# Retention's output in buffers of its own, branch A's finish on VectorE one block per pair of heads, and 32-row tiles for sample states and gate's low-rank rows

## What is computed

```python
z = rmsnorm(x) @ w_in                               # 1024 -> 6944 columns
za, zb, ga, gb = z[:SHIFT_W], z[SHIFT_W:...], ...   # branch A, branch B, two merge gates
# branch A: RWKV-7, 8 heads of 64
zs = za + mu * (shift(za) - za)
r, k, v, dw, da, dg = split(zs)                     # dw 64, da 64, dg 160 columns: low rank
decay = exp(-exp(-softplus(-(w0 + tanh(dw) @ lw_up)) - 0.5))
a = sigmoid(a0 + da @ la_up)
g = sigmoid(dg) @ lg_up                             # 160 -> 512
S = S * decay - (S kk) b^T + v k^T;  y_t = S r_t     # over tokens, done in chunks of 64
ya = (head_norm(y) * gain + bias + (r . k r_k) v) * g
# branch B: retention, 8 heads, keys of 64, values of 128
o = chunkwise_retention(rotary(q), rotary(k) / 8, v, S_ret)
yb = head_norm(o) * silu(gate)
x = x + rmsnorm((sigmoid(ga) * (ya @ w_out_a) + sigmoid(gb) * (yb @ w_out_b)) @ w_o)
x = x + rmsnorm((silu(h @ w_gate) * (h @ w_up)) @ w_down)          # h = rmsnorm(x)
```

## Time and profile before

| | |
|---|---|
| median of 3 runs | 1299.23 us (1298.85 to 1300.09) |
| profiled execution | 1297.91 us |
| its span in the trace | 1296.1 us, 27750 instructions |
| mean granted TensorE clock | 0.984 of 2.4 GHz |
| TensorE busy (matmul) | 1234.4 us, 95% |
| VectorE, ScalarE, GpSimd busy | 859.7, 556.0 and 157.5 us (66%, 43%, 12%) |
| DMA | 179.52 MB, mean 139 GB/s |

### The profile page before, as it was taken

The page is one execution under the profiler, slowest core; times in us unless marked ns, Lnnn a source line. Parts: engine busy times, 40 slices in busy tenths (PEclk is TensorE's granted clock), DMA queues, the critical chain, the costliest instruction groups (busy, mean ns, idle before and its releaser), DMA issues.

```text
span 1296.1 us, 27750 instructions
## 1 busy us (share of the span) xinstructions
PE 1234.4 (95%) x11992; PEld 1163.6 (90%) x11992; DVE 859.7 (66%) x1444; ACT 556.0 (43%) x849; POOL 157.5 (12%) x168
## 2 busy tenths in 40 slices
PE   6999999899998999999899998998999989999996
PEld 5899887899998999999898987877999989999996
DVE  4887559877776665653487954787877666566433
ACT  5553334354435433343444533344444453333432
POOL 0004463300000000000000071831100000000000
PEclk9999999999999999999999999998999989999998
DMA  6333144644453545444433423255454434444441
GB/s 227 130 108 125 53 119 145 224 139 146 139 163 116 190 148 151 155 148 147 130 115 114 132 68 82 91 184 179 141 167 132 157 107 148 154 154 144 150 149 72
DMA packets 51178, 179.52 MB, mean 139 GB/s; under 512 B 6256, under 2 KB 7024, under 8 KB 49776
## 3 DMA queue, kind: packets, MB, share of 16 engines
q1 hardware_dynamic: 42576, 153.77, 37.6%
q10 hardware_dynamic: 8480, 23.97, 5.2%
HBM read 166.57 MB, written 8.53 MB: 135 GB/s over the span
## 4 chain that ended last, share of the span: by engine, by line
PE 83%; DVE 9%; POOL 3%; ACT 2%; issue 2%; DMA 1%; SPq 0%; ACTq 0%; DVEq 0%; POOLq 0%
PE dense L1368 51%; PE core L1368 32%; DVE w_lo L898 2%; ACT w_hi L599 1%; POOL qk_rot L530 1%; POOL rot_tmp L528 1%; POOL qk_rot L527 1%; DVE x L947 1%; DVE y_out L945 1%; DMA qk_rot<-qk_raw 1%; DMA x<-x_t 0%; POOL s_st L541 0%; DVE ya_lo L926 0%; DVE bonus L1016 0%; DVE tmp L1002 0%
## 5 line engine op out<-in xcount | busy, mean ns | idle before, releaser
L898 DVE TENSOR_TENSOR w_lo<-w_raw,w_hi 128x1024 fp32r<-128x1024 f32 x282 | 358.2, 1272 | 228.4 <-ACT w_hi L599 227.9
L599 ACT ACTIVATE w_hi<-w_raw 128x1024 fp32r<-128x1024 f32 x282 | 297.5, 1056 | 445.2 <-PE dense L1368 294.0
L1368 PE MATMUL dense<-h_hi,w_hi 128*128 128x320 f32 x1296 | 416.9, 322 | 23.4 <-DVE h_lo L902 11.8
L1368 PE MATMUL dense<-h_lo,w_hi 128*128 128x320 f32 x1296 | 404.9, 312 | 1.1 <-issue 1.1
L1368 PE MATMUL dense<-h_hi,w_lo 128*128 128x320 f32 x1296 | 404.8, 312 | 0.0
L1368 PEld LDWEIGHTS dense<-h_hi,w_hi 128*128 128x128 f32 x1296 | 247.0, 191 | 43.8 <-issue 36.9
L1368 PEld LDWEIGHTS dense<-h_lo,w_hi 128*128 128x128 f32 x1296 | 247.4, 191 | 2.7 <-issue 1.5
L1368 PEld LDWEIGHTS dense<-h_hi,w_lo 128*128 128x128 f32 x1296 | 247.4, 191 | 0.0
L1368 PE MATMUL core<-h_hi,w_hi 128*128 128x320 f32 x416 | 129.3, 311 | 0.0
L1368 PE MATMUL core<-h_lo,w_hi 128*128 128x320 f32 x416 | 128.8, 310 | 0.0
L1368 PE MATMUL core<-h_hi,w_lo 128*128 128x320 f32 x416 | 128.7, 309 | 0.0
(11 more groups left out here) (299 smaller groups left out, 2004.3 us busy)
## 6 DMA issues: line engine op xcount, KB each, us to landing
w_raw<-wts SPq DMA_DIRECT2D x282, 512.0 KB, 3.5
ret_t<-ret_t ACTq DMA_DIRECT2D x16, 256.0 KB, 3.8
ret_s<-ret_t ACTq DMA_DIRECT2D x16, 256.0 KB, 2.8
ret_rest<-ret_d ACTq DMA_DIRECT2D x2, 1536.0 KB, 7.5
qk_rot<-qk_raw SPq DMA_DIRECT2D x8, 320.0 KB, 6.1
dmask<-rconst ACTq DMA_DIRECT2D x2, 1152.0 KB, 5.8
s_st<-wkv_st ACTq DMA_DIRECT2D x2, 1024.0 KB, 5.0
wkv_s<-s_st ACTq DMA_DIRECT2D x2, 1024.0 KB, 7.2
```

The lines of the kernel that those rows point to most:

```text
L599: act.activation(w_hi[n % RING][:, :], w_raw[n % RING][:, :], ACT.Copy).then_inc(hi_ready.sem, 1)
L898: dve.tensor_tensor(w_lo[r][:, :], w_raw[r][:, :], w_hi[r][:, :].bitcast(F32), ALU.subtract).then_inc(low_made.sem, 1)
L1368: return pe.matmul(out, lhsT, rhs, start=start, stop=stop)
```

## The change

Four things are changed.

- Low-rank: the input weights of gate's last 32 low-rank columns are given four times side by side, so that the last chunk of `zs` holds them in each of its four groups of 32 rows, and `lora_w` (1152 columns) holds the four output blocks' weights in those groups. TensorE first makes the four 128-row products, then the four 32-row ones, each in a row group of its own.
- Sample states: `v_exp` and `u_exp` are 256 columns, a group of 32 rows holding four sequences; a state is made by eight matmuls on tiles of 32 rows x 64 columns into four banks. All four steps use the same four banks, each waits for the evacuation of the one before, and the order in `TAIL` is another.
- Finish of branch A: GpSimd's part is gone; each pair of branch B's heads has VectorE finish one block (product, sum, split), behind its fourth tile's evacuation.
- Branch B's output stands in four buffers of its own, `o_pair`, with two for the squares, so that `y_a` and `sq_a` stay.

```diff
-TAIL = [("gate", 0), ("s", 0), ("mean", 0), ("mean", 1), ("s", 1), ("gate", 1), ("mean", 2), ("mean", 3), ("s", 2), ("s", 3),
-        ("var", 0), ("var", 1), ("gate", 2), ("var", 2), ("var", 3)]
+TAIL = [("gate", 0), ("s", 0), ("mean", 0), ("mean", 1), ("s", 1), ("gate", 1), ("s", 2), ("mean", 2), ("mean", 3), ("gate", 2),
+        ("var", 0), ("var", 1), ("s", 3), ("var", 2), ("var", 3)]
...
-        o_b, sq_b = at("o_b", 70, 2560), at("sq_b", 99, 2560)
+        o_pair = [at(f"o_pair{hp}", kb, 2 * T) for hp, kb in enumerate((92, 20, 24, 28))]
+        sq_pair = [at("sq_pair0", 99, 2 * T), at("sq_pair1", 101.5, 2 * T)]
...
-        def state_banks(h):
-
-            return (core[3], core[2]) if h % 2 else (dense[2], core[4])
+        of_u, of_v = (dense[2], core[3]), (core[4], core[2])
...
@@ GpSimd, at the start of pair 0
-                    if hp == 0:
-                        pool.wait_ge(*root_a(layer, 1))
-                        pool.wait_ge(*bonus_gated(layer, HP))
-                        pool.wait_ge(*y_gated(layer, HP))
-                        finish_ya(0)
-                        finish_ya(1)
...
-                    act.activation(zs[0:32, 2 * T:3 * T], zs[0:32, 2 * T:3 * T], ACT.Sigmoid).then_inc(lora_act.sem, 1)
+                    act.activation(zs[:, 2 * T:3 * T], zs[:, 2 * T:3 * T], ACT.Sigmoid).then_inc(lora_act.sem, 1)
...
@@ VectorE, evacuation of a sample state
-                        link(dve.tensor_tensor(st, st, state_banks(h)[0][:, :], ALU.add))
-                        dve.tensor_tensor(st, st, state_banks(h)[1][:, :], ALU.add).then_inc(seq_evac.sem, 1)
+                        for q in range(2):
+                            part = st[:, 256 * q:256 * q + 256]
+                            link(dve.tensor_tensor(part, part, of_v[q][:, 0:256], ALU.add))
+                            ins = dve.tensor_tensor(part, part, of_u[q][:, 0:256], ALU.add)
+                            if q == 0:
+                                link(ins)
+                        ins.then_inc(seq_evac.sem, 1)
...
                 def finish_ya(i):
-                    dve.wait_ge(*ya_sum(layer, i // 2 + 1))
+                    if i == 0:
+                        dve.wait_ge(*root_a(layer, 1))
+                        dve.wait_ge(*bonus_gated(layer, HP))
+                        dve.wait_ge(*y_gated(layer, HP))
+                    y = ch(y_a, i)
+                    link(dve.tensor_tensor(y, y, ch(sq_a, i), ALU.mult))
+                    link(dve.tensor_tensor(y, y, ch(bonus, i), ALU.add))
                     split(ch(ya_hi, i), ch(ya_lo, i), ch(y_a, i)).then_inc(ya_ready.sem, 1)
...
@@ VectorE, in each pair hp of branch B
-                    if hp == 0:
-                        finish_ya(0)
-                        gate(nxt)
-                        finish_ya(1)
-                    else:
-                        gate(nxt)
+                    gate(nxt)
+                    if hp:
                         finish_yb(hp - 1)
...
-                    if hp == 0:
-                        for i in (2, 3):
-                            finish_ya(i)
-                        dve.wait_ge(*ya_ready(layer, HP))
                     gate(nxt + 2)
                     low(layer, fill + 2)
                     gate(nxt + 3)
+                    finish_ya(hp)
                     low(layer, fill + 3)
...
                     elif g == T_GATE + 6:
-                        pe.wait_ge(*seq_evac(layer, EVAC_AT["s2", SAMPLE]))
+                        pe.wait_ge(*seq_evac(layer, EVAC_AT["s3", SAMPLE]))
...
@@ TensorE, lora_mm n
                         mm(ps, lora_w[:, 512 + c:512 + c + 128], zs[:, T:2 * T], True, False)
-                        ins = mm(ps, lora_w[0:32, 1024 + c:1024 + c + 128], zs[0:32, 2 * T:3 * T], False, True)
+                        if n == len(LORA) - 1:
+                            for m in range(8, len(LORA)):
+                                rows = slice(32 * (LORA[m] - 8), 32 * (LORA[m] - 8) + 32)
+                                mm(core[m % 5][:, 0:T], lora_w[rows, 1024:1152], zs[rows, 2 * T:3 * T], False, True).then_inc(lora_done.sem, 1)
+                        return
...
@@ TensorE, sample_state(h)
                     if h == 0:
                         pe.wait_ge(*v_tok_ready(layer, 8))
-                        evac("ys", NCHUNK - 1)
-                    elif h == 1:
                         evac("y", SAMPLE)
                     else:
-                        evac(f"s{h - 2}", SAMPLE)
+                        evac(f"s{h - 1}", SAMPLE)
                     tk = step_mats(tok, SAMPLE, 128)[:, h, :]
-                    of_u, of_v = state_banks(h)
-                    across(of_v[:, :], tk[:, 0:C], v_exp[h % 2][:, :])
-                    done(halves(of_u[:, :], tk[:, C:2 * C], u_exp[h % 2][:, :]))
+                    for of, keys, spread, crossed in ((of_v, tk[:, 0:C], v_exp, 1), (of_u, tk[:, C:2 * C], u_exp, 0)):
+                        for q in range(2):
+                            for half in range(2):
+                                rows, to = slice(C * half + 32 * q, C * half + 32 * q + 32), C * (half ^ crossed)
+                                ins = mm(of[q][to:to + C, 0:256], keys[rows], spread[h % 2][rows, :])
+                    done(ins)
```

More of the change, by code:

```diff
@@ L186, in program @@
         tok = at("tok", 50, 2560)
-        lora_w = at("lora_w", 60, 1536)
+        lora_w = at("lora_w", 60, 1152)
         ar = at("ar", 60, 2560)
@@ L229, in program, with o_of, sq_of @@
         up_g = [at("up_g0", 74, T), at("up_g1", 76, T)]
+        def o_of(i):
+            return o_pair[i // 2][:, i % 2 * T:(i % 2 + 1) * T]
+        def sq_of(i):
+            return sq_pair[i // 2 % 2][:, i % 2 * T:(i % 2 + 1) * T]
         dense = [ctx.enter_context(nc.psum_tensor(f"dense{i}", [128, 512], F32)) for i in range(3)]
@@ L543, in _ @@
                     rotate(i)
[L545 to L551, removed]
                 for hp in range(HP):
@@ L1090, in spread @@
                 def spread(h, to, of):
-                    return dve.tensor_tensor(to[h % 2][:, :].rearrange("p (s c) -> p s c", s=NSEQ), bc(of, 1, NSEQ),
-                                             bc(fx[:, F_SEQ:F_SEQ + NSEQ], 2, C), ALU.mult)
+                    return dve.tensor_tensor(to[h % 2][:, :].rearrange("p (s c) -> p s c", s=4), bc(of, 1, 4),
+                                             bc(fx[:, F_SEQ:F_SEQ + 4], 2, C), ALU.mult)
                 def make(name):
                     h = int(name[1])
-                    if h == 0:
-                        dve.wait_ge(*v_turned(layer, 7))
                     if h >= 2:
@@ L1222, in finish_yb @@
                     for i in (2 * hp, 2 * hp + 1):
[L1223 to L1224 removed]
+                        o = o_of(i)
+                        link(dve.scalar_tensor_tensor(o, o, vec("gnb_g", i), sq_of(i), ALU.mult, ALU.mult))
                         if i == 0:
@@ L1718, in variances @@
                     for par in range(2):
-                        mm(core[3 + par][:, 0:T], ones, ch(sq_b, 2 * hp + par)).then_inc(var_b.sem, 1)
+                        mm(core[3 + par][:, 0:T], ones, sq_of(2 * hp + par)).then_inc(var_b.sem, 1)
                 pe.wait_ge(*rotated(layer, 8))
@@ L1887, in tiles, with four @@
         return w.reshape(DEPTH, KT, 128, -1, 128).transpose(0, 3, 2, 1, 4).reshape(DEPTH, -1, 128, KT * 128)
+    def four(q):
+        return np.concatenate([q] + [q[:, :, -32:]] * 3, 2)
     w = v["w_in"]
     a, r0 = A_W, SHIFT_W
-    parts = [w[:, :, 3 * a:SHIFT_W], w[:, :, a:2 * a], w[:, :, 0:a], w[:, :, 2 * a:3 * a], w[:, :, r0:]]
+    parts = [four(w[:, :, 3 * a:SHIFT_W]), w[:, :, a:2 * a], w[:, :, 0:a], w[:, :, 2 * a:3 * a], w[:, :, r0:]]
     ts = [tiles(q) for q in parts]
@@ L1902, in za @@
     def za(q):
-        q = np.concatenate([np.pad(q[:, :, 3 * a:], ((0, 0), (0, 0), (0, 3 * 128 - (SHIFT_W - 3 * a)))),
+        q = np.concatenate([four(q[:, :, 3 * a:]),
                             q[:, :, a:2 * a], q[:, :, 0:a], q[:, :, 2 * a:3 * a]], 2)
@@ L1910, in layout @@
     up = np.concatenate([v["lora_w_up"], v["lora_a_up"]], 1)
-    lg = np.pad(v["lora_g_up"], ((0, 0), (0, 96), (0, 0))).reshape(DEPTH, 2, 128, A_W).transpose(0, 2, 1, 3).reshape(DEPTH, 128, -1)
-    lora = np.concatenate([up, lg], 2)
+    lg = v["lora_g_up"]
+    last = lg[:, 128:].reshape(DEPTH, 32, 4, 128).transpose(0, 2, 1, 3).reshape(DEPTH, 128, 128)
+    lora = np.concatenate([up, lg[:, :128], last], 2)
     x_t = np.concatenate([v["x_prompt"].reshape(TP, D), v["x_sample"].reshape(TS, D)], 0)
```

20 lines of the change are left out of this document (9 added, 11 removed).

## The result

The changed kernel takes 1284.33 us (median of 4 runs, 1279.92 to 1286.61), the one before 1299.04 us in the same comparison: a ratio of 0.9891, 95% interval 0.9875 to 0.9908.

A forecast was written before the change was run, and what follows sets the result against it. TensorE, with 83% of the chain, was taken as the bound. Terms -5.4 + 0.6 - 2.4 - 4.4 = -11.6 from 1297.91 give 1286.3; with 1.3 for the median, 1287.6 us, range 1283.8 to 1294.5.

The forecast's parts named there:

- Low-rank, -5.4: Gate's low-rank matmuls: the block takes 2.95 instead of 5.67 us, -2.7 us a layer, all passed on.
- the rival of serial tiles: 32-row tiles in different row groups run one after another: a state takes 3.4 us, total 1312.2; chance 0.04.
- Sample states, +0.6: Branch A's tail: states of 0.65 us, but evacuation stalls eat the saving; 0 in layer 0, +0.6 in layer 1.
- a second stall was forecast there, at state 2: Layer 1's tail: state 2 waits for state 1's evacuation, ending near 854.7; last gate tile begins at 863.3, against 862.68.
- The finish, -2.4: Branch B's pairs: pair 0's wait shrinks, -2.9 us a layer; VectorE's 1.8 us blocks add new stalls in later pairs.
- The new waits were forecast as 2.0 and 1.4 us: Stalls for ret_t in pairs 1 and 2: 1.4 and 0.6 us in layer 0, 0.6 and 0.8 in layer 1.
- behind pair 3 the price was set to 0: Behind branch B's pair 3: the block costs 0, since TensorE waits for ScalarE's and VectorE's last work anyway.
- The clock, -4.4: Behind branch B's pair 0: with shorter stalls the clock stays at 2.4 GHz, saving 1.6 and 2.8 us, or 0 if not.
- a rival, with stalls of 1.4 us: The granted clock falls all the same or at another place, pairs with such new stalls being near it: 1292.0; chance 0.20.

The follow-up runs named there:

- e1: The kernel before with the low-rank part of the change alone: 1291.46 us, ratio 0.9954 to the kernel before.
- e7: The changed kernel with branch A's finish blocks at earlier places in their pairs and the tail in another order: 1275.43 us, 0.9813 of the kernel before.
- e5: The kernel before with 64 waits on a passed semaphore added to TensorE's queue in layer 0's pair 1: 0.9973 of the kernel before, 3.5 us faster.
- e10: The kernel before with 64 waits on a passed semaphore ahead of layer 0's FFN and 64 behind it: 0.9943 of the kernel before.
- e6: The changed kernel with six more linked VectorE operations in pair 0's finish block: 1292.8 us, 0.9953 of the kernel before.
- e3: The kernel before with only branch B's separate buffers and branch A's finish on VectorE: 1294.85 us, 0.9975 of the kernel before.
- e9: The changed kernel with 96 waits on a passed semaphore ahead of layer 0's FFN and 96 behind it: 0.9889 of the kernel before.
- e12: The kernel before with 128 waits on a passed semaphore ahead of layer 0's FFN and 128 behind it: 0.9979 of the kernel before.

## Why the prediction came out as it did

- **Low-rank, -5.4:** right. The block went from 5.67 to 2.90 us, the saving passed on, and e1 measures 6.0. The four 32-row matmuls overlap; the rival of serial tiles is refuted by the state's 0.62 us too.
- **Sample states, +0.6:** right within 1 us in its own stage. A state is 0.62 us (0.65 taken), the wait at state 1 is there with 1.56 and 1.22 us (1.2 to 1.5 taken), and the tail as a whole gave -0.3, less than the 1 us by which the old tail differs between traces. Layer 1's share was read wrongly: a second stall was forecast there, at state 2, and none came. The Trainium skill (TensorEngine Tiling (Array Packing), PSUM Bottleneck) warns that tiling speeds up TensorE but not the evacuation, and the trace agrees as far as that goes. But this change also made the evacuation longer, 1.8 us for 1.3, and let all states share four banks, and no run separates the three. e7, which puts a tile between the two uses of the banks, has no wait.
- **What the part did elsewhere, 0:** the largest miss. No step of the sum has it, because each counted a change only where its own instructions stand. The 16 more matmuls a layer moved layer 1's instructions in TensorE's queue, and a shift alone is worth 3.5 us (e5) to 7.4 (e10).
- **The finish, -2.4:** too good, by 1.8 us in the profile of the changed kernel. Pair 0 gave 2.85 and 2.86 us, as forecast (2.9), and the block's 1.8 was right. The new waits were forecast as 2.0 and 1.4 us. The pairs' lengths give 0.68 + 1.38 + 0.87 = 2.9 in layer 0, and in layer 1, without the clock, 1.89 + 0.69 + 0.88 = 3.5. The projections behind pair 3 give back 0.35 and 0.94, so in all -0.6. Two steps were off. ScalarE was taken to deliver `w_hi` as in the rows of before; in this execution it was late twice, which makes the 1.38 and the 1.89. And behind pair 3 the price was set to 0 because TensorE waits there anyway; the pair is 0.9 us longer, and only a part of that comes back.
- **The clock, -4.4:** the mechanism was right (e6), and so was the size behind pair 0, where the falls are gone (1.6 and 2.7 us by the lengths of pairs 1, 4.4 on average over eight traces). In this execution one of 1.6 came behind the 1.80 us wait at the end of layer 1's pair 1: -2.7. The prediction had that as a rival, with stalls of 1.4 us; in e3's trace waits of 1.62 and 1.52 us at such places brought no fall.

The forecast terms of the finish and the clock add to -6.8. Four pairs and projections of both layers together, against the first profile of before, give -3.4 in the changed kernel, -4.6 in e3 and -6.9 in e9, where no wait for `ret_t` is over 0.61 (there less the 0.75 us that its own waits add ahead of layer 0's FFN). So the two terms hold in the best execution and fall short by up to half in others. e3's timed -3.2 (1.3 to 5.2) can't settle it, since its one profile has the longest chunk stage of all, 91.68 us.

That the total came near is in part luck. Without the 3.5 to 7.4 us of the shift, which had no term, the changed kernel would be 7 to 11 us faster (an estimate from its 14.7), which is still inside the range but less than the 11.6 forecast. What the finish and the clock fell short by was made up by something that the prediction did not know of.

**What stays open.** That a place in the queue matters is shown; why is not. The gaps without a releaser fit instruction fetches that come at a bad moment in a stage of short matmuls, but no row ties a fetch to a gap, and the one rule tried for it failed. What held ScalarE's store up in some executions and not in others isn't known either. Nor is it known why layer 0's stage, at 79.8 to 82.7 us in all fourteen traces, never shows the long form.

## What to carry to other kernels

Time a change against a control that only moves the instructions behind it: here 64 waits on a passed semaphore were worth as much as a part of the change. When work moves to an engine with slack, put it where that engine waits, not where it is late: the same block cost 6 us more at the one place than at the other. When matmuls get faster and share banks, the evacuation of the bank is next, so give it a tile of cover. And before a term is called wrong on one profile, read the same stretch in the profiles of the other kernels.

## What the runs showed of the hardware

- TensorE's gaps without a releaser depend on where a stretch of short matmuls stands in its queue: the gaps over 1 us add to 6.8 to 7.4 us in layer 1's chunk stage unshifted (5 traces, the stage 87 to 91.7 us), to 1.6 to 4.0 us shifted (9 traces, 81 to 84.2 us). The granted clock fell in that stage in all five, and in three of the nine (e6, e9, e12).
- A wait of TensorE of 3.45 us or more in branch B was followed by a granted clock of 1.2 GHz in 18 cases of 18, waits of 0.67 us or less at the same place in none.
- Eight fp32 matmuls on 32x64 tiles, 256 columns each, leave 16 records in 0.62 us; four on 64x64 tiles with 512 columns leave 8 in 1.02 us.
- A switch between 128-row and 32-row loads leaves the loader idle for 0.44 us; eight such switches in a block of 5.67 us, two in one of 2.90.
- Waits on a passed semaphore are not free once there are many: 64 of them left a wait of 3.72 us as it was (e10), 96 made it 4.47 and 4.56 (e9), 128 made it 6.28 (e12).
